# Scores of the following group issued between a group's transposes and its product with the values

## What is computed

```python
s = jnp.einsum('bhqd,bhkd->bhqk', q, k) * scale + bias      # masked, causal
p = jax.nn.softmax(s, axis=-1)
o = jnp.einsum('bhqk,bhkd->bhqd', p, v)
# difference attention, c = 0, 1:
a = (p[:, :, 0] - lam * p[:, :, 1]).astype(v.dtype)
o = jnp.einsum('bhqk,bhkd->bhqd', a, v)
return rmsnorm(o, subln_g) * (1.0 - lam_init)
```

## Time and profile before

| | us |
|---|---|
| median of 3 runs | 3202.05 |
| lowest and highest run | 3198.3 and 3203.61 |
| the profiled execution's own time | 3196.35 |
| its span | 3194.5 |
| TensorE busy | 2969.4 (93% of the span) |
| VectorE busy | 1423.3 (45%) |
| ScalarE busy | 947.8 (30%) |
| GpSimd busy | 442.2 (14%) |
| all DMA, 293.82 MB | 92 GB/s mean |

### The profile page before, as it was taken

One profiled execution on the slowest core, in us unless ns is written; L12 is line 12 of the kernel. 1 busy time (PEld: TensorE's weight loads), 2 busy tenths in 40 slices (PEclk: granted clock), 3 DMA queues, 4 the chain that ended last, 5 costly groups with the idle time before them and its releaser, 6 DMA issues.

```text
span 3194.5 us, 32580 instructions
## 1 busy us (share of the span) xinstructions
PE 2969.4 (93%) x13570; PEld 2371.3 (74%) x13570; DVE 1423.3 (45%) x2222; ACT 947.8 (30%) x1260; POOL 442.2 (14%) x345
## 2 busy tenths in 40 slices
PE   5888877899999899999999998889999988999998
PEld 5766755778888788887888875668888865588886
DVE  5266553365753433334232444444435444545353
ACT  2223243232122322224222332333222323332222
POOL 1010110121011221222101100011102100022022
PEclk8879898899999999999999999989999999999999
DMA  5212200044632222222442221112232310222321
GB/s 203 90 48 72 92 15 26 27 173 166 246 137 94 89 83 83 83 76 84 128 146 97 94 83 55 60 50 99 77 115 76 115 55 25 79 93 81 110 85 67
DMA packets 49810, 293.82 MB, mean 92 GB/s; under 512 B 6473, under 2 KB 6601, under 8 KB 23808
## 3 DMA queue, kind: packets, MB, share of 16 engines
q1 hardware_dynamic: 43056, 272.94, 24.0%
q0 software_dynamic: 4736, 15.43, 1.8%
q10 hardware_dynamic: 1872, 3.37, 0.3%
HBM read 283.07 MB, written 8.65 MB: 91 GB/s over the span
## 4 chain that ended last, share of the span: by engine, by line
PE 85%; DVE 7%; ACT 5%; issue 1%; DMA 1%; POOL 0%; DVEq 0%; ACTq 0%; POOLq 0%
PE ps L211 85%; DVE ada L392 2%; DVE wlo L204 1%; ACT F L1037 1%; PE ps L1061 1%; DMA Rf<-in_ada0h 1%; DVE F L349 0%; DVE F L1073 0%; ACT whi L193 0%; ACT hh L362 0%; DVE hl L353 0%; ACT L246 0%; DVE F L1898 0%; DMA cst<-in_const 0%; DVE F L1049 0%
## 5 line engine op out<-in xcount | busy, mean ns | idle before, releaser
L211 PE MATMUL ps<-hh,whi 128*128 128x512 f32 x2080 | 831.9, 400 | 43.5 <-DVE hl L353 19.7
L211 PE MATMUL ps<-hl,whi 128*128 128x512 f32 x2080 | 819.3, 394 | 0.0
L211 PE MATMUL ps<-hh,wlo 128*128 128x512 f32 x2080 | 819.2, 394 | 0.0
L204 DVE TENSOR_TENSOR wlo<-raw,whi 128x2048 fp32r<-128x2048 f32 (+2 forms) x235 | 492.0, 2093 | 547.8 <-ACT whi L193 542.7
L211 PE MATMUL ps<-R,whi 128*128 128x512 f32 x2080 | 651.1, 392 | 7.8 <-DVE wlo L204 2.8
L193 ACT ACTIVATE whi<-raw 128x2048 fp32r<-128x2048 f32 (+2 forms) x235 | 408.6, 1739 | 723.4 <-PE ps L211 723.4
L211 PEld LDWEIGHTS ps<-hh,whi 128*128 128x128 f32 x2080 | 396.7, 191 | 139.6 <-issue 43.7
L211 PEld LDWEIGHTS ps<-R,whi 128*128 128x128 f32 x2080 | 391.1, 188 | 95.7 <-issue 7.2
L211 PEld LDWEIGHTS ps<-hl,whi 128*128 128x128 f32 x2080 | 396.0, 190 | 84.5
L211 PEld LDWEIGHTS ps<-hh,wlo 128*128 128x128 f32 x2080 | 396.8, 191 | 81.2 <-issue 1.4
L211 PE MATMUL ps<-R,wlo 128*128 128x512 f32 x1040 | 405.1, 390 | 0.0
(11 more groups left out here) (251 smaller groups left out, 2504.3 us busy)
## 6 DMA issues: line engine op xcount, KB each, us to landing
F<-in_ada SPq DMA_DIRECT2D x36, 1024.0 KB, 4.8
raw<-in_fs0in SPq DMA_DIRECT2D x22, 1024.0 KB, 5.3
raw<-in_fs1in SPq DMA_DIRECT2D x22, 1024.0 KB, 4.7
raw<-in_fc0in SPq DMA_DIRECT2D x22, 1024.0 KB, 4.8
raw<-in_fc1in SPq DMA_DIRECT2D x22, 1024.0 KB, 4.8
Rf<-in_ada0h SPq DMA_DIRECT2D x24, 512.0 KB, 3.5
raw<-in_fs0out SPq DMA_DIRECT2D x16, 704.0 KB, 4.5
raw<-in_fs1out SPq DMA_DIRECT2D x16, 704.0 KB, 4.0
```

The costliest lines, as they stand in the source:

```text
L204: e.tensor_tensor(m.wlo[n % 2][:, 0:size], m.raw[n % 3][:, 0:size], m.whi[n % 2][:, 0:size].bitcast(F32), SUB).then_inc(*s.up("wlo", n))
L211: return e.matmul(out, l, r, start=start, stop=stop, skip_group_check=True)
```

## The change

The product with the values becomes a step of its own, "pv", in both lists. Before, it was the end of step t; now it comes behind the scores of the following group, and the copies to the output (`act_out`, `dve_out`) move with it. The functions of all engines follow. SP and POOL issue what they did, in the same order.

```diff
--- before.py
+++ after.py
@@ -1120,6 +1120,7 @@
 
 def h64_order():
 
+
     yield from (("qk", 0), ("v", 0), ("v", 1), ("a", 0), ("a", 1))
     for h in range(8):
         if h % 2 == 0 and h < 6:
@@ -1129,6 +1130,7 @@
         yield "t", h
         if h < 6:
             yield "a", h + 2
+        yield "pv", h
 
 
 def pe_h64(e, s, m, st):
@@ -1159,11 +1161,12 @@
                 s.wait_ge(V_BY[1], st, 1, 3)
             a, rows = h64_qk(m, p), slice(64 * hh, 64 * hh + 64)
             pe_scores(e, s, m, g, [(a[rows, 0:T], a[rows, T:2 * T])])
+        elif what == "t":
+            for t in range(4) if i == 0 else ():
+                s.wait_ge(V_BY[t % 2], st, 1, t)
+            pe_turn(e, s, m, h64_group(st, i))
         else:
             g, (p, hh) = h64_group(st, i), divmod(i, 2)
-            for t in range(4) if i == 0 else ():
-                s.wait_ge(V_BY[t % 2], st, 1, t)
-            pe_turn(e, s, m, g)
             if hh == 0 and p:
                 s.wait_ge("o_lo_dve", st, p - 1)
             pe_values(e, s, m, g, lambda c: values[:, c, 64 * i:64 * i + 64], m.ps[7][64 * hh:64 * hh + 64, :])
@@ -1187,8 +1190,9 @@
             act_tok(e, s, m, st, n, i, values)
         elif what == "a":
             act_scores(e, s, m, h64_group(st, i))
+        elif what == "t":
+            act_turn(e, s, m, h64_group(st, i))
         else:
-            act_turn(e, s, m, h64_group(st, i))
             if i % 2:
                 act_out(e, s, m, st, i // 2, (st, i))
 
@@ -1237,8 +1241,9 @@
             dve_scores(e, s, m, g, m.f(A_BIAS + T * (i % 2)))
             dve_recip(e, s, m, g)
             dve_weights(e, s, m, g)
+        elif what == "t":
+            dve_turn(e, s, m, h64_group(st, i))
         else:
-            dve_turn(e, s, m, h64_group(st, i))
             if i % 2:
                 dve_out(e, s, m, st, i // 2, (st, i))
 
@@ -1325,6 +1331,8 @@
             for t in range(4) if i == 0 else ():
                 s.wait_ge(V_BY[t % 2], "diff", 1, t)
             pe_turn(e, s, m, g)
+        elif what == "pv":
+            g = diff_group(i, 0)
             if i:
                 s.wait_ge("sub", i - 1, 0)
             pe_values(e, s, m, g, lambda c: values[:, c, P * i:P * i + P], m.ps[7][:, :])
@@ -1352,7 +1360,7 @@
                 act_scores(e, s, m, diff_group(i, n))
         elif what == "t":
             act_turn(e, s, m, diff_group(i, 0))
-        else:
+        elif what == "norm":
             s.wait_ge("pv", "diff", i, 0)
             if i:
                 s.wait_ge("sub", i - 1, 1)
```

## The result

The changed kernel takes 3151.49 us (median of 4 runs, 3147.68 to 3154.87) against 3202.83 us for the kernel before (4 runs, 3198.3 to 3204.83): 51.3 us less, a ratio of 0.984 with an interval of 0.982 to 0.986. The forecast was 3150 us, with a range of 3136 to 3168.

A forecast was written before the change was run, and what follows sets the result against it. TensorE carries the chain for 85% of the span, losing time to waits and lower clock because scores come late. Even head stage 18.3, odd 22.0, difference stage 11.7 sum to 52.0 us: 3202 to 3150 us, range 3136 to 3168.

The forecast's parts named there:

- The waits and their cause: Odd half of head-stage periods: TensorE waits 1.68 and 1.14 us because scores reach VectorE and ScalarE late; ScalarE wait becomes about 0.4.
- The period: Head stages, two heads turn to turn: 24.15 us at full clock; three periods 72.45, saving 18.3 (even stage) and 22.0 (odd).
- The output copies cost nothing: Head stages: odd heads' output copies behind exponentials and weights are covered by over 10 us of projection; without cover, 0.69 us.
- The difference stage: Scores and square 2.82 us earlier, 1.56 us idle left; saves 8.5 us if the clock falls, 14.9 if it holds, middle 11.7.
- The sum: Whole kernel: 18.3 + 22.0 + 11.7 = 52.0 us gained, from 3202 to 3150 us.
- The last head's bonus: Difference stage, last head: about 5 us more gain if its values and reduction also run at full clock.
- A: Head stages: waits go but the clock still falls once per period, 17 us lost; gain 35, or 32, 3170 us; 12%.
- B: Head stages: clock stays low from first turn to projection, period 34.7 us; kernel slower at 3216 us; 4%.
- C: No change, 3202 us: VectorE or a slab replaces the wait (weights late for the next turn), or order unfelt; 3%.

## Why the prediction was right

By its own steps:

1. **The waits and their cause.** Right. The odd half's waits fell from 1.68 and 1.14 us to 0.42, with the same number of instructions on every engine, and ScalarE turned from late to early. The order of TensorE alone did it, as the run with the output copies ahead shows.
2. **The period.** Forecast 24.15 us, measured 24.4. The failed term is the start of the first scores: I let them start 1.74 us into the turn, and they start at 1952.20 - 1950.30 = 1.90. Of these 0.16 us, 0.09 to 0.10 is the overlap, which I had taken from the latent stage: a score matmul here starts 0.08 us before the recorded end of the transposes (1951.59 + 0.69 = 1952.28), not 0.17. The other 0.07 us is the three transposes' own, recorded for 0.69 us where the earlier trace rows have 0.62. The rest is a few hundredths each: values reach to the next step in 2.30 us instead of 2.26, twice, and the odd half's turn takes 2.19 instead of 2.15. The projection is as forecast, 11.01 us. Six periods make 146.4 for 144.9: the head stages gave 38.9 us, not 40.3.
3. **The output copies cost nothing.** Right: three periods take 73.21 us with the copies in either place.
4. **The difference stage.** The square came when forecast and the idle is 1.48 us for 1.56. The clock held over it in all three heads that have it, so the reductions run at the full level: the upper of my two bounds, where I took the middle. Head 0 saved 29.91 - 24.92 = 5.0, head 1 28.74 - 23.29 = 5.45, head 2, at the difference of the totals, 2.8: 13.2 us, against 8.5 and 14.9 for the bounds and 11.7 for my value. Head 0 missed its 6.6 since behind its reduction the clock fell after all, for eight projection matmuls of 0.63 to 0.67 us (24.92 - 23.29 = 1.6 us more than head 1). Where it held behind head 0 too, in the run with the scores ahead of the turn, the difference stage took 2120.47 - 2060.28 = 60.19 us from first turn to last, 14.9 us less than before: the upper bound as forecast. A stretch behind head 0 of the changed kernel, at the lower level:

```profile
2038.00:2039.00 1.00, 1.00 (x4) 0.81 (x3) 1.00 (x3) 0.11 (x1) 0.00 (x0) 0.50 0.00 0
```

5. **The sum.** 52.0 us forecast; 52.1 in the changed stages, 51.3 in the medians. That it is so close is partly luck: the head stages gave 1.4 us less and the difference stage 1.5 more.
6. **The last head's bonus**, some 5 us if it ran at full clock too, wasn't to be had: the clock falls over the 2.10 us before its turn, and the turn takes 1.76 us, values 4.64. In the run with the difference stage alone the same turn, behind the same 2.10 us, took 0.98 us, but it won nothing, since the clock fell in the wait that follows:

```profile
2107.95 0.98 PE L1061 MATMUL ps<-cst,F 128*128 128x128 f32 x7 [2.10 <-DVE F L1404]
2110.49 0.90 PE L1061 MATMUL ps<-cst,F 128*128 128x128 f32 x3 [1.55 <-ACT F L1078]
2111.77 4.63 PE L211 MATMUL ps<-F 128*128 128x512 f32 x8 [0.38 <-DVE F L1073]
```

The bonus was also priced too high: with these pauses filled and the clock at 1.00, the last head gave 2.5 us, half of what I had put on it.

The rivals. A (waits go, clock still falls) and B (transposes and half-array matmuls keep it low) are excluded by the 1.00 of both stages, which the filled old order has as well. The Trainium skill, "TensorE: Matmul & The Clock Gate", Part 4, says that the full clock does not engage for transposes. These runs disagree as far as a stage goes that mixes them with matmuls: seven transposes in 0.93 us, at a granted 1.00. No run here was made of transposes alone. C (no gain) had asked for weights that are late for the next turn; no such wait is in the trace of after.

## What to carry to other kernels

When engines execute in order, a step's place decides not only when it runs but what it stands in front of on the other engines. Follow the consumer: here scores behind the turn and ahead of the values gave 24.4 us a period, scores behind the values 30.3 to 31.5, and scores ahead of the turn 34.3 to 35.7. Price a pause of TensorE at its length plus what the lower clock costs afterwards, which doubled it here; where a pause can't be removed, another step of the program moved into it is worth most, and even matmuls on constants paid (17.5 us of the whole kernel in the old order).

## What was not expected of the hardware

The clock's share, 19.8 of 38.9 us, was larger than the idle time it came from seemed to justify: 17.5 us of the whole kernel came back by adding work and removing none. In each of the six periods of the kernel before, the granted clock fell between the end of the first pause, 1.68 us, and the end of the second, some 1.1 us, and stayed low for some 7 us or, once, 14.

The difference stage shows how little the length of a pause says. The changed order of heads 0 and 1, with 1.48 us of idle before the reduction and 0.78 behind it, was profiled five times (the change and its repeat, the difference stage alone, the output copies first, the scores first). No execution lost the clock in the 1.48 us. Around the 0.78 us it fell in head 0 in four of the five and in head 1 in none. With the 2.10 us before the last head's turn, in these five and in the run with the reduction inside the projection, it fell all six times: five times within the pause and once in the next wait, of 1.55 us. What decides the case of head 0, which has the same code and the same pauses as head 1, these runs don't show.
